# Expert rounds of a fused two-model kernel: even block placement, a last round summed from PSUM, gate rows formed in the convolution stage

## The chip, the cores and the metric

The kernel runs on one core of a Trainium2 chip. The metric is device time in microseconds (us) of the whole program, one launch.

## The reference, cut to what matters

Two transformer-like blocks run one after the other on 256 tokens of width 1024, all in fp32. The second block has two layers. Each layer is a mixer (attention in layer 0, a short convolution in layer 1), and then a mixture of experts with 32 experts in 4 groups, of which each token uses 2. Only the 256 latent tokens are routed here, so each layer has 512 (token, expert) pairs.

```python
x = x + g1 * mixer(modulate(x, ...))
f = modulate(x, norm_ffn_g, sh2, sc2)            # 256 rows of 1024
# _hier_moe: group = argmax(g_prob + b), 2 experts of its 8, weights w
y[token] = sum over its 2 experts e of
           w * ((silu(f @ w_gate[e]) * (f @ w_up[e])) @ w_down[e])
x = x + g2 * y
...
return rmsnorm(x, final_norm_g)                   # after layer 1
```

An expert has three matrices of 2 MB (1024x512, 1024x512, 512x1024), so 6.3 MB an expert and 201 MB a layer. `g1` and `g2` are rows of 1024 gates, the same for all tokens.

## The kernel before, in words

The five engines each have a program of their own, and semaphores tie them together. SyncE (SP) issues the loads of weights, in a fixed order. GpSimd (POOL) issues the gathers and scatters of rows and some small loads. TensorE (PE) multiplies, VectorE (DVE) and ScalarE (ACT) move data from PSUM and do the elementwise work.

**The first block's feed-forward part (`ffn0`)** has 22 steps. In each step TensorE makes an up product (`up`) and the down product of the step before (`down(t - 1)`, which waits for `gated`). VectorE scales, convolves and gates, and then does one `mod_pass`: a pass over a 2 MB chunk of `w_mod`, which POOL loads (`mod_loads`, one chunk ahead of the pass, two buffers).

**Blocks.** Behind the router, the rows of each expert are cut in blocks of 32 slots. Each expert has at least one block. There are 48 blocks (`NB`), three to a round (`WIDE`), so 16 rounds (`ROUNDS`). If the experts need `total` blocks, `48 - total` are free, and expert `e` starts at block

```python
pst[e] = start[e] + ((NB - total) * e >> 5)      # start[e]: blocks of the experts before e
```

which spreads the free blocks by the number of the expert. A free block belongs to the expert before it and holds no rows. `route` computes this on VectorE, in operations of 32 columns that each wait for the one before (L2332 to L2335), from products of TensorE with the counts. A second chain (L2354 to L2358) gives each expert's end on 32 partitions, for the table `tab_i`.

**Rounds (`experts`).** The weights of three experts fit in SBUF (`experts3`, expert `e` in place `e % 3`). SP loads expert by expert in this order: gate matrix of `e`, down matrix of `e - 1`, up matrix of `e`. Each half of a matrix waits (L775) until the last round that uses expert `e - 3` has finished the same half (`quarter_done`). A round multiplies its 96 gathered rows by the gate, up and down matrix of its three blocks, each matrix in four quarters. The first block's weights are read in place, those of the second are copied by VectorE (L2400) and those of the third by ScalarE (L1684). VectorE waits until the matrices of the expert of the third block have landed. Behind the down product VectorE multiplies the 96 rows with the gates `g2` into `ym` (L2408), and POOL scatters them to the DRAM tensor `y_rows` by slot (L2775).

**After the rounds.** SP waits for the last scatter, then fetches `y_rows` into `y01` (`fetch`, L812), and `combine` adds both rows of each token to the residual in 8 operations (L2448, L2449). ScalarE squares each half as it is combined, VectorE sums them (L1962), and the norm goes on. In layer 0 the gate rows of layer 1 are formed at the same place: `row_diags` makes three 128x1024 operands on VectorE (L2213), `row_pair` makes six products on TensorE and six copies on ScalarE (L1656). Then comes the convolution's stage: 8 steps of 24 products on TensorE (L843), and a short chain on VectorE for each.

## Time and profile before

| | |
|---|---|
| Median of 3 runs | 2247.38 us (2246.84 to 2250.01) |
| Profiled execution, its time | 2246.04 us |
| Profiled execution, its span | 2244.2 us |
| TensorE busy | 1929.4 us (86%) |
| VectorE busy | 956.4 us (43%) |
| ScalarE busy | 665.8 us (30%) |
| DMA | 617.69 MB, mean 275 GB/s |
| Rounds of layer 0 | about 1066 to 1554 us |
| Rounds of layer 1 | about 1731 to 2219 us |

The span is the time from the first to the last record of the profiled execution, 1.8 us less than its own time. TensorE's busy time is that of its matmul records, which overlap.

### The profile page before, as it was taken

Reading aid. Unit: us, or ns where it says so; the run is one execution under the profiler, and the core shown is the slowest. Engines: PE = TensorE matmul, PEld = TensorE weight load, DVE = VectorE, ACT = ScalarE, POOL = GpSimd, SP = SyncE. Lnnn points to the kernel's source line nnn. Section 1 sums busy time; section 2 is a strip of 40 time slices with the busy share of each in tenths; the row PEclk is TensorE's granted clock in tenths of the full one; section 3 lists DMA queues with packets and bytes.
Section 4 is the critical chain, followed back from the end, with each engine's and each line's share of the span. In section 5 each row is a group of like instructions: output and inputs, shape, how many; then the busy total and the mean of one; then the engine's idle time right before and its main releaser. Section 6 shows DMA issues by size and latency. Waiting matters only on the chain.

```text
span 2244.2 us, 29502 instructions
## 1 busy us (share of the span) xinstructions
PE 1929.4 (86%) x9453; PEld 1085.2 (48%) x9454; DVE 956.4 (43%) x2077; ACT 665.8 (30%) x1053; POOL 100.0 (4%) x133
## 2 busy tenths in 40 slices
PE   8878999999999999997976887777897967877885
PEld 4534777745577775554432433333764423323332
DVE  2273888312478534444432432334224423323333
ACT  1142000012400002132543543444102534434443
POOL 2000000000000000000000000000000000000000
PEclk9869999999899999998998998999997988888998
DMA  8502898433179543305899999996645999999994
GB/s 282 201 6 99 325 343 312 178 141 143 66 277 358 197 167 132 124 31 207 334 421 383 360 412 407 407 416 260 258 160 221 385 421 379 415 421 389 411 394 166
DMA packets 84611, 617.69 MB, mean 275 GB/s; under 512 B 16289, under 2 KB 16609, under 8 KB 21809
## 3 DMA queue, kind: packets, MB, share of 16 engines
q1 hardware_dynamic: 68912, 544.70, 61.3%
q0 software_dynamic: 14752, 69.77, 8.3%
q10 hardware_dynamic: 864, 2.19, 0.2%
q8 instruction: 44, 0.72, 0.1%
q14 instruction: 39, 0.31, 0.0%
HBM read 621.84 MB, written 19.92 MB: 286 GB/s over the span
## 4 chain that ended last, share of the span: by engine, by line
PE 67%; DMA 19%; DVE 5%; issue 3%; ACT 3%; DVEq 2%; SPq 1%; ACTq 0%; POOLq 0%
PE ps L843 25%; PE ps L1216 15%; PE ps L1053 14%; DMA big<-in_w_up 7%; PE ps L1065 7%; DMA big<-in_w_down 5%; DMA big<-in_w_gate 5%; PE ps L1218 3%; PE ps L857 2%; ACT big L1684 2%; DVEq L2413 1%; DVE hT L2421 1%; PE ps L1245 1%; DMA c_res<-f_rows,big 1%; PE ps L1208 1%
## 5 line engine op out<-in xcount | busy, mean ns | idle before, releaser
L1216 PE MATMUL ps<-big,hT 128*32 128x512 f32 x3072 | 723.5, 627 | 144.0 <-ACT big L1684 140.5
L1218 PE MATMUL ps<-big,hT 128*32 x1536 | 722.3, 627 | 0.0
L1684 ACT COPY big<-big 128x1024 f32 x384 | 395.0, 1046 | 526.2 <-PE ps L1218 267.1
L2400 DVE TENSOR_SCALAR big<-big 128x1024 f32 x384 | 263.0, 696 | 623.0 <-PE ps L1218 375.6
L1216 PEld LDWEIGHTS ps<-big,hT 128*32 128x32 f32 x3072 | 200.5, 114 | 541.3 <-DVE big L2400 276.0
L1053 PE MATMUL ps<-hT,big 128*128 128x256 f32 x1408 | 311.1, 379 | 0.0
L843 PE MATMUL ps<-big,hT 128*128 128x512 f32 (+4 forms) x792 | 299.7, 537 | 4.8 <-DMA big<-in_dense 2.5
L1053 PEld LDWEIGHTS ps<-hT,big 128*128 128x128 f32 x1408 | 266.7, 190 | 49.0 <-issue 14.8
L843 PEld LDWEIGHTS ps<-big,hT 128*128 128x128 f32 x792 | 144.4, 195 | 149.3 <-issue 139.7
L843 PE MATMUL ps<-big 64*30 64x256 f32 (+14 forms) x704 | 161.4, 512 | 30.7 <-DVE big L2350 8.3
L1218 PEld LDWEIGHTS ps<-big,hT 128*32 128x32 f32 x1536 | 164.8, 114 | 6.1 <-issue 0.9
L1065 PE MATMUL ps<-big 128*128 128x512 f32 x352 | 159.2, 595 | 0.4 <-DVE big L2163 0.4
L2173 DVE SCALAR_TENSOR_TENSOR big<-big,s_ccol 128x512 f32<-128x512 f32 x196 | 147.4, 752 | 7.0
L1648 ACT ACTIVATE big<-big 128x256 f32<-128x256 f32 x44 | 18.3, 417 | 363.8 <-DVE big L2155 363.8
L843 PEld LDWEIGHTS ps<-big 64*128 64x128 f32 (+8 forms) x704 | 81.7, 196 | 90.3 <-issue 63.1
L843 PE MATMUL ps<-hT,big 128*128 128x256 f32 (+1 forms) x480 | 112.8, 398 | 1.9 <-ACT hT L1897 1.9
L843 PEld LDWEIGHTS ps<-hT,big 128*128 128x128 f32 x480 | 92.4, 193 | 22.7 <-issue 10.7
L1065 PEld LDWEIGHTS ps<-big 128*128 128x128 f32 x352 | 66.1, 190 | 72.9 <-issue 69.0
L2137 DVE TENSOR_TENSOR big<-ps,big 128x512 f32<-128x512 f32 x44 | 30.4, 690 | 119.5 <-PE ps L1053 117.5
L1245 PE MATMUL ps<-c_ident,hT 96*128 96x96 f32 x128 | 29.5, 318 | 50.4 <-DVE hT L2421 50.4
L857 PE MATMUL ps<-c_ident,big 128*128 128x128 f32 (+4 forms) x349 | 57.4, 301 | 17.6 <-DVE big L2085 10.9
L2764 POOL DMA_INDIRECT c_res<-f_rows,big x32 | 32.5, 1014 | 715.4 <-PE ps L1208 486.7
(333 smaller groups left out, 1176.2 us busy)
## 6 DMA issues: line engine op xcount, KB each, us to landing
big<-in_w_down SPq DMA_DIRECT2D x128, 1024.0 KB
big<-in_w_gate SPq DMA_DIRECT2D x128, 1024.0 KB, 12.1
big<-in_w_up SPq DMA_DIRECT2D x128, 1024.0 KB, 12.9
big<-in_dense SPq DMA_DIRECT2D x52, 1536.0 KB, 8.3
big<-in_dense POOLq DMA_DIRECT2D x28, 2048.0 KB, 9.9
big<-in_dense SPq DMA_DIRECT2D x21, 2048.0 KB, 8.3
big<-in_dense SPq DMA_DIRECT2D x5, 1024.0 KB, 7.5
big<-y_rows SPq DMA_DIRECT2D x4, 1024.0 KB, 6.2
```

Source lines behind the costliest of these rows:

```text
L843: ins = nc.tensor.matmul(out, lhsT, rhs, start=start, stop=stop)
L857: ins = nc.tensor.transpose(out, rows, const["ident"][0:k, 0:k])
L1053: ins = nc.tensor.matmul(ps[:, t % 2, f * S:(f + 1) * S], w[:, k, f * P:(f + 1) * P], hT[:, k, S:2 * S], start=k == 0, stop=k == KT - 1)
L1065: ins = nc.tensor.matmul(ps[:, 4 + 2 * c + h, :], gT[:, t % 2, c * P:(c + 1) * P], w[:, h * BW:(h + 1) * BW], start=t == 0, stop=t == FT - 1)
L1216: nc.tensor.matmul(ps[g * SLOTS:(g + 1) * SLOTS, bank, :], xT[:, k, g * SLOTS:(g + 1) * SLOTS], side[:, g - 1, quarter % 2, at:at + BW], s ...
L1218: return nc.tensor.matmul(ps[0:SLOTS, bank, :], xT[:, k, 0:SLOTS], experts3[:, bass.ds(here, 1), kind * CH + row:kind * CH + row + BW] .re ...
L1245: ins = nc.tensor.transpose(ps[:, 4 + 3 * h, k * ROWS:(k + 1) * ROWS], rows, const["ident"][0:ROWS, 0:ROWS])
L1684: nc.scalar.copy(side[:, 1, quarter % 2, :], experts3[:, bass.ds(there, 1), lo:lo + QW] .rearrange("p a n -> p (a n)")).then_inc(s["side2_ ...
L2137: tt(U[:, par, :, 2:S + 2], ps[:, par, :].rearrange("p (a b) -> p a b", a=2), token_scale, mult)\
L2173: ins = stt(acc, mod_w[j % 2][:, k, :], ccols[:, k, col:col + 1], acc, mult, add)
L2400: ts(side[:, 0, quarter % 2, :], experts3[:, bass.ds(there, 1), lo:lo + QW].rearrange("p a n -> p (a n)"), 1.0, None, mult).then_inc(s["si ...
L2764: nc.gpsimd.indirect_dma_start(out=xe, out_offset=None, in_=f_rows[:, :], in_offset=bass.IndirectOffsetOnAxis(ap=token_i[:, b:b + 1], axis=0),
```

## The change

The diff has four parts.

1. **Even placement.** Expert `e` starts at block `start[e] + min(lead[e], NB - total)`, where `lead[e]` is the largest `3 * e' // 2 - start[e']` over `e' <= e`. So an expert isn't placed ahead of one and a half blocks per expert as long as free blocks are left. The running maximum takes five shifted `max` operations; the second chain becomes one `tensor_tensor_reduce`, and three small products of TensorE go.
2. **Rows of the last round.** 15 rounds are scattered. Their rows are fetched during the last round (the fetch waits for the scatter of round 14 and for the last round's first matrix) and added to the residual. The last round's rows are then written to `ym` in two halves, multiplied by a one-hot matrix `hot` (four products), and added from PSUM. Since some rows of `y_rows` are no longer written, there is one tensor per layer, and both are filled with zeros in `ffn0`: eight writes of 512 KB by POOL, which waits for them before it goes on to `mod_loads`.
3. **Gate rows** of layer 1 are formed in steps 0 to 2 of the convolution's stage, whose products now use 6 PSUM banks; `row_diags` comes after the scaling of the stage's input.
4. The loads of `conv_in` stand behind the fetch in SP's order and so can be issued during the last round too. `final_g` is loaded after the last round's second matrix.

```diff
-    r[:, 1] = e
-    r[:, 2] = (np.arange(P) + 1)[:, None]
+    r[:, 1] = WIDE * e // 2
+    r[np.arange(E - 1), 2, e[1:]] = 1.0
+    r[E - 1, 2, E - 1] = 2 * NB
...
@@ fetch (SP)
-                after(sp, "moe" + tag)
+                sp.wait_ge(m["y_stored"].sem, m["y_stored"].end)
+                sp.wait_ge(m["quarter_done"].sem, m["quarter_done"].at(12 * (ROUNDS - 1) + 4))
...
@@ route (PE)
-                mm(ps[0:E, 4, 0:1], rt[0:E, 0, :], nbT[0:E, 0:1], True, False)
-                mm(ps[0:E, 4, 0:1], const["ident"][0:E, 0:E], nbT[0:E, 0:1], False, True)
-                mm(ps[0:E, 4, 1:2], const["ones"][0:E, 0:E], nbT[0:E, 0:1], True, True, s["route_pe"].sem)
...
@@ experts (PE), after the last turn
+                pe.wait_ge(m["hot_ready"].sem, m["hot_ready"].end)
+                for c in range(T):
+                    for h in range(2):
+                        if c == 0:
+                            pe.wait_ge(m["last_ready"].sem, m["last_ready"].at(h + 1))
+                        mm(ps[:, 2 * c + h, :], hot[0:ROWS, c, :], ym[0:ROWS, h * BW:(h + 1) * BW], True, True,
+                           m["last_spread"].sem)
...
@@ between the expert stage and normX2 (PE), and in conv
-            for j in range(3):
-                row_pair("g1_1", j, 2 * j)
-            after(pe, "g1_1")
...
+                if t < 3:
+                    if t:
+                        g = st["g1_1"]["gate_copied"]
+                        pe.wait_ge(g.sem, g.at(2 * t))
+                    row_pair("g1_1", t, CONV_BANKS)
...
@@ ffn (DVE), ffn0 alone
+                if name == "ffn0":
+                    nc.vector.memset(zeros, 0.0).then_inc(st["zero"]["zeros_ready"].sem, 1)
...
@@ route (DVE)
-                L(ts(rest[:, 0:E], ps[:, 3, E:2 * E], -1.0, float(NB), mult, add))
-                L(tt(pad_i[:, 0:E], rest[:, 0:E], rt[:, 1, :], mult))
-                L(ts(pad_i[:, 0:E], pad_i[:, 0:E], E.bit_length() - 1, None, ALU.logical_shift_right))
-                L(tt(pst, ps[:, 3, 0:E], pad_i[:, 0:E], add))
+                first = SHIFTS[-1]
+                ts(rest, ps[:, 3, E:E + 1], -1.0, float(NB), mult, add)
+                L(tt(lead[:, 0, first:], rt[:, 1, :], ps[:, 3, 0:E], sub))
+                for i, n in enumerate(SHIFTS):
+                    old, new = lead[:, i % 2, :], lead[:, 1 - i % 2, :]
+                    L(tt(new[:, first:], old[:, first:], old[:, first - n:first - n + E], ALU.max))
+                L(stt(pst, lead[:, len(SHIFTS) % 2, first:], rest, ps[:, 3, 0:E], ALU.min, add))
...
@@ experts (DVE), after the last turn; combine() goes
-                rows_out(ROUNDS - 1)
+                link(v, nc.vector.tensor_copy(last_token, token_i[:, ROUNDS - 1:ROUNDS]))
                 for c in range(T):
+                    ins = ts(hot[0:ROWS, c, :], const["iota"][0:ROWS, :], float(c * P), last_token[0:ROWS, :], add, ALU.is_equal)
+                ins.then_inc(m["hot_ready"].sem, 1)
+                if layer == 0:
+                    mod_gains(1, 0)
+                for out, c, h in parts:
+                    if h == 0:
+                        v.wait_ge(m[f"y_fetched_{c}"].sem, m[f"y_fetched_{c}"].end)
+                    link(v, tt(out, out, y01[:, c, 0, h * BW:(h + 1) * BW], add))
+                    link(v, tt(out, out, y01[:, c, 1, h * BW:(h + 1) * BW], add))
+                v.wait_ge(done.sem, done.end)
+                v.wait_ge(s["y_stored"].sem, s["y_stored"].end)
+                for h in range(2):
+                    cols = slice(h * BW, (h + 1) * BW)
+                    tt(ym[0:ROWS, cols], ps[0:ROWS, 5 + h, :], gb2[0:ROWS, 0, cols], mult).then_inc(m["last_ready"].sem, 1)
+                for i, (out, c, h) in enumerate(parts):
+                    v.wait_ge(m["last_spread"].sem, m["last_spread"].at(i + 1))
+                    tt(out, out, ps[:, 2 * c + h, :], add).then_inc(m["combined"].sem, 1)
...
@@ POOL
+            s = st["zero"]
+            pool.wait_ge(s["zeros_ready"].sem, s["zeros_ready"].end)
+            for l in range(DEPTH):
+                for q in range(4):
+                    pool.dma_start(y_rows[l][q * P:(q + 1) * P, :], zeros).then_inc(s["rows_zeroed"].sem, 16)
+            pool.wait_ge(s["rows_zeroed"].sem, s["rows_zeroed"].end)
             mod_loads(0, "normF0")
```

## Rows read from the trace of the kernel before

**Rows 1.** Stretches of layer 0's rounds: length, busy by engine, TensorE clock, DMA share, GB/s

```profile
1190.00:1224.00 34.00, 27.24 (x165) 11.40 (x162) 10.87 (x17) 13.61 (x15) 2.01 (x2) 0.87 0.92 359
...
1276.00:1289.00 13.00, 11.51 (x84) 5.42 (x78) 5.96 (x8) 7.73 (x8) 1.01 (x1) 1.00 0.60 202
1289.00:1397.00 108.00, 84.45 (x526) 37.30 (x525) 35.60 (x55) 45.46 (x51) 7.06 (x7) 0.91 1.01 415
...
1538.00:1554.00 16.00, 14.76 (x100) 7.39 (x94) 5.44 (x9) 7.25 (x8) 0.00 (x0) 1.00 0.10 41
```

**Rows 2.** The same view, rounds of layer 1

```profile
1856.00:1889.00 33.00, 26.81 (x161) 10.91 (x158) 10.10 (x16) 13.62 (x15) 2.00 (x2) 0.87 0.91 347
...
2031.00:2062.00 31.00, 25.44 (x162) 10.82 (x159) 10.63 (x17) 13.67 (x16) 1.06 (x2) 0.93 0.95 366
...
2200.00:2219.00 19.00, 17.75 (x125) 8.95 (x118) 7.52 (x12) 9.93 (x10) 0.00 (x0) 1.00 0.07 29
```

**Rows 3.** Order of time, SP's loads of expert weights around 1282 us

```profile
1282.81 3.75 SPq L767 DMA_DIRECT2D big<-in_w_gate  x2
```

**Rows 4.** Order of time, VectorE, L2408 (start, duration): ends of rounds

```profile
1254.43 1.22 DVE L2408 TENSOR_TENSOR c_res<-ps,hT 96x1024 f32<-96x1024 f32 x1
...
1279.07 1.21 DVE L2408 TENSOR_TENSOR c_res<-ps,hT 96x1024 f32<-96x1024 f32 x1
...
2171.68 1.21 DVE L2408 TENSOR_TENSOR c_res<-ps,hT 96x1024 f32<-96x1024 f32 x1
...
2196.51 1.21 DVE L2408 TENSOR_TENSOR c_res<-ps,hT 96x1024 f32<-96x1024 f32 x1
...
2219.53 1.22 DVE L2408 TENSOR_TENSOR c_res<-ps,hT 96x1024 f32<-96x1024 f32 x1 [2.63 <-PE ps L1218]
```

**Rows 5.** Order of time, layer 0, from the last round to the norm

```profile
1550.82 0.69 DVE L2400 TENSOR_SCALAR big<-big 128x1024 f32 x1 [1.02 <-PE ps L1218]
...
1554.14 1.22 DVE L2408 TENSOR_TENSOR c_res<-ps,hT 96x1024 f32<-96x1024 f32 x1 [2.63 <-PE ps L1218]
...
1564.20 0.69 DVE L2448 TENSOR_TENSOR x_res<-x_res,big 128x512 f32<-128x512 f32 x1 [0.83 <-DMA big<-y_rows]
...
1572.73 0.16 DVE L1962 TENSOR_TENSOR sums<-ssq_x 128x2 f32<-128x2 f32 x1 [2.49 <-ACT big L1565]
```

**Rows 6.** Order of time, layer 1, the same sum

```profile
2237.12 0.16 DVE L1962 TENSOR_TENSOR sums<-ssq_x 128x2 f32<-128x2 f32 x1 [0.79 <-ACT big L1565]
```

**Rows 7.** By stretch, as rows 1: after the rounds of layer 0

```profile
1554.00:1560.00 6.00, 0.11 (x1) 0.00 (x0) 1.79 (x3) 0.00 (x0) 1.10 (x2) 0.79 0.03 10
...
1562.00:1564.00 2.00, 2.00 (x4) 0.96 (x3) 1.34 (x3) 0.59 (x1) 0.09 (x1) 0.50 1.01 410
```

**Rows 8.** Groups of TensorE instructions, 1577 to 1665 us (convolution)

```profile
L843 PE MATMUL ps<-hT,big 128*128 128x256 f32 x384 | 84.9, 385 | 1.9 <-ACT hT L1897 1.9
```

**Rows 9.** Order of time, route, layer 0

```profile
1049.33 0.19 DVE L2335 TENSOR_TENSOR big<-ps,big 128x32 f32<-128x32 f32 x1
1049.55 0.22 DVE L2337 SCALAR_TENSOR_TENSOR big<-big,ps 128x64 f32<-128x64 f32 x1
```

**Rows 10.** Order of time, ffn0, VectorE: mod pass 1, gate of step 2

```profile
240.34 0.48 DVE L2171 TENSOR_SCALAR big<-big,s_ccol 128x512 f32<-128x512 f32 x1
...
249.38 0.43 DVE L2163 TENSOR_TENSOR big<-big 128x256 f32<-128x256 f32 x1
```

**Rows 11.** Chain that ended last, in order of time: ffn0 (start, duration)

```profile
254.54 3.43 PE ps L1065 x8
```

**Rows 12.** The page, DMA issues: count, KB each, median us to landing

```profile
big<-in_dense POOLq DMA_DIRECT2D x28, 2048.0 KB, 9.9
...
f_rows<-big ACTq DMA_DIRECT2D x4, 512.0 KB, 8.3
...
out_x<-x_res SPq DMA_DIRECT2D x2, 512.0 KB, 2.7
```

**Rows 13.** Order of time, ffn0, POOL: load of mod chunk 2

```profile
237.23 0.54 POOL L2786 DMA_DIRECT2D big<-in_dense  x1 [16.70 <-DVE big L2173]
```

More of the change, by code:

```diff
@@ L209, in two_blocks @@
         f_rows = nc.dram_tensor("f_rows", [S, D], fp32, kind="Internal").ap()
-        y_rows = nc.dram_tensor("y_rows", [2 * S, D], fp32, kind="Internal").ap()
+        y_rows = [nc.dram_tensor(f"y_rows{l}", [2 * S, D], fp32, kind="Internal").ap() for l in range(DEPTH)]
         def area(lo, *shape, parts=P):
@@ L387, in two_blocks @@
         side = area(3 * CH, 2, 2, QW)
-        y01 = area(2048, TC, 2, D)
+        y01 = area(0, TC, 2, D)
+        hot = hflat[:, 3584:3584 + TC * P].rearrange("p (c n) -> p c n", c=TC)
+        last_token = hflat[:, 3584 + TC * P:3584 + TC * P + 1]
+        zeros = area(6144, D)
         gb2 = hflat[:, 2560:2560 + D].rearrange("p (a d) -> p a d", a=1)
@@ L422, in two_blocks @@
         nbT = area(RB + 1768, P)
-        rest = area(RB + 1896, E + 1)
-        pad_i = area(RB + 1929, E + 1).bitcast(i32)
+        SHIFTS = tuple(1 << i for i in range(E.bit_length() - 1))
+        lead = area(RB + 2680, 2, SHIFTS[-1] + E)
+        rest = area(RB + 2776, 1)
+        next_at = area(RB + 1896, E)
         pst = area(RB + 1962, E)
@@ L1164, in route @@
                 e = st["ent" + name[-1]]
-                pe.wait_ge(g2["diag_done"].sem, g2["diag_done"].end)
+                pe.wait_ge(g2["gate_diags"].sem, g2["gate_diags"].end)
                 pe.wait_ge(e["turned_a"].sem, e["turned_a"].end)
                 for h in range(2):
-                    mm(ps[:, 7 - h, :], const["ones"][:], diag2[:, 4 * h:4 * h + 4, :], True, True, g2["banks_ready"].sem)
+                    mm(ps[:, 7 - h, :], const["ones"][:], diag2[:, 4 * h:4 * h + 4, :], True, True, g2["gate_ready"].sem)
                 pe.wait_ge(s["route_dve"].sem, s["route_dve"].at(4))
@@ L1791, in _ @@
             ffn("ffn0")
+            after(act, "zero")
             s = st["normA1"]
@@ L1887, in _ @@
             after(act, "moe0")
-            for j in range(3):
-                row_pair("g1_1", j, 2 * j)
-            after(act, "g1_1")
             combined_squares("comb0", "normX2")
             root("normX2", rstd_x)
-            token_scales("normX2", 6)
+            token_scales("normX2", 2)
             s = st["normX2"]
@@ L2219, in entry @@
                 g1, g2 = st["g1_" + tag], st["g2_" + tag]
-                v.wait_ge(g1["act_evac"].sem, g1["act_evac"].end)
+                v.wait_ge(g1["gate_copied"].sem, g1["gate_copied"].end)
                 tt(diag2, const["ident"][:].unsqueeze(1).broadcast_to([P, KT, P]),
-                   mod[:, layer, 5 * KT:6 * KT, 0].unsqueeze(2).broadcast_to([P, KT, P]), mult).then_inc(g2["diag_done"].sem, 1)
+                   mod[:, layer, 5 * KT:6 * KT, 0].unsqueeze(2).broadcast_to([P, KT, P]), mult).then_inc(g2["gate_diags"].sem, 1)
                 v.wait_ge(r["aux_loaded"].sem, r["aux_loaded"].end)
@@ L2226, in entry @@
                 nc.vector.tensor_reduce(swS, swK.rearrange("p k n -> p n k"), AX.X, add).then_inc(r["route_dve"].sem, 1)
+                nc.vector.memset(lead[:, :, 0:SHIFTS[-1]], 0.0)
                 nc.vector.tensor_copy(vals[:, :, 1], const["tokid"][:])
@@ L2351, in route @@
                 ins.then_inc(step, 1)
+                L(nc.vector.tensor_tensor_reduce(out=next_at[0:E, :], in0=pst[0:E, :], in1=rt[0:E, 2, :], scale=1.0,
+                                                 scalar=0.0, op0=mult, op1=add, accum_out=pend[0:E, :]))
+                ts(past[0:E, :], const["iota"][0:E, 0:NB], pend[0:E, :], None, ALU.is_ge).then_inc(step, 1)
                 v.wait_ge(s["route_pe"].sem, s["route_pe"].at(7))
[L2354 to L2359 removed]
                 nc.vector.tensor_copy(slot_w, ps[:, 6, 2 * ROUNDS:3 * ROUNDS])
@@ L2437, in experts @@
                     turn(b)
-                rows_out(ROUNDS - 1)
-            def combine(name, T, x):
-                s = st[name]
+                m = st["comb" + name[-1]]
+                parts = [(lat(c)[:, h * BW:(h + 1) * BW], c, h) for c in range(T) for h in range(2)]
+                link(v, nc.vector.tensor_copy(last_token, token_i[:, ROUNDS - 1:ROUNDS]))
                 for c in range(T):
-                    v.wait_ge(s[f"y_fetched_{c}"].sem, s[f"y_fetched_{c}"].end)
-                    for h in range(2):
-                        cols = slice(h * BW, (h + 1) * BW)
-                        out = x(c)[:, cols]
-                        link(v, tt(out, out, y01[:, c, 0, cols], add))
-                        tt(out, out, y01[:, c, 1, cols], add).then_inc(s["combined"].sem, 1)
+                    ins = ts(hot[0:ROWS, c, :], const["iota"][0:ROWS, :], float(c * P), last_token[0:ROWS, :], add, ALU.is_equal)
[15 more added lines that the diff above has]
+                    tt(out, out, ps[:, 2 * c + h, :], add).then_inc(m["combined"].sem, 1)
             gains = small["gcols"][:].rearrange("p (i k) -> p i k", k=KT)
@@ L2552, in _ @@
             ffn("ffn0", "normF0")
+            after(v, "zero")
             for h in range(2):
@@ L2818, in _ @@
             moe("moe0", "1", 1)
-            after(pool, "moe1")
+            d = st["moe1"]["quarter_done"]
+            pool.wait_ge(d.sem, d.at(12 * (ROUNDS - 1) + 8))
             aux("final", [(fg_row, dram["final_g"])])
```

76 lines of the change are left out of this document (39 added, 37 removed).

## The prediction

> **What bounds the kernel now.** I read the busy times by stretch first. In the rounds of both layers DMA is the bound: between 1289 and 1397 us its share is 1.01 and it moves 415 GB/s, while TensorE's records cover 84 of 108 us [rows 1]. A round needs two new experts on average (32 experts, 16 rounds), 12.6 MB of weights and 0.8 MB of rows. At 415 GB/s that is 32 us. A round whose weights are there takes 24.6 us: from 1254.43 to 1279.07 [rows 4]. So the end of a layer is the time at which DMA is through, plus a tail, and something inside the rounds is worth time only where it fills a hole of DMA or shortens the tail.
>
> The same view shows the holes. In layer 0 the share is 0.92 for 34 us and 0.60 for 13 us, which against 1.01 is 34 x 0.09 = 3.1 and 13 x 0.41 = 5.3, together 8.4 us [rows 1]. In layer 1 it is 0.91 for 33 us and 0.95 for 31 us, 3.3 + 1.9 = 5.2 us [rows 2]. The order of SP's loads tells what a hole is: the gate matrix issued at 1282.81 [rows 3] comes at the second quarter of the round that began at 1279 [rows 4], when the queue had run dry. All three places for experts were taken, and none was free before that round.
>
> The tails: DMA is through at about 1539.5 in layer 0 (share 0.10 from 1538 to 1554) [rows 1], and the last product ends at 1554.1 [rows 5], so 14.6 us. In layer 1 it is through at about 2200 (0.07) [rows 2], and the last product ends at 2219.5 [rows 4], so 19.5 us.
>
> Last I read the chain and the order of time around the places that change: from the last round to the norm [rows 5, 6], the convolution [rows 8], and `ffn0` [rows 10, 11].
>
> **Even placement.** The routing isn't in the trace, so I ran the reference's router on its inputs: 36 blocks are needed in either layer, 12 are free; layer 0 has one expert of three blocks and two of two, layer 1 has four of two. By the old rule 3 rounds of layer 0 and 10 of layer 1 reach beyond expert 2r + 1 in round r (one of layer 1 by two experts), so three new or nearly new experts meet in one round, and another round needs only one. By the new rule no round of either layer does. While a round uses three experts all places are taken and SP can only follow TensorE by the quarter; with two, the third place takes loads a round ahead (five matrices, 25 us of DMA at 415 GB/s, can be queued behind a gate matrix). I take the holes as filled by four fifths: of 8.4 + 5.2 = 13.6, 11 us. The bound below is nothing: another hole can open, for instance where layer 0 now has the rounds (12, 12, 12) and (13, 14, 15). Above it is all 13.6 and some 3 us of smaller holes.
>
> The tail of layer 1 is a second gain. Its last two rounds ran at the pace of the engines, 24.8 and 23.0 us [rows 4], behind a round that had to wait for expert 28's down matrix (26, 27, 28). It becomes (26, 27, 27), and the last round can start when expert 31's gate matrix lands, as in layer 0. I take layer 0's tail, 14.6 for 19.5: 5 us, between 0 and 5. Together **-16** (0 to -22).
>
> **Route.** On VectorE four linked operations of 32 columns become an unlinked one and seven linked ones. From 1049.33 to 1049.55 is one link, 0.22 us [rows 9]. So 7 x 0.22 + 0.1 - 4 x 0.22 = 0.76 us a layer, in front of the first gather, which the first round waits for. The second chain and the three products lay beside TensorE's 128-column products and are worth nothing; put ahead of the wait, the reduce stays in the same cover. **+1.5** for both layers (0 if the gather's wait behind expert 2's weights hides it, 2 at most).
>
> **Rows of the last round.** Before, in layer 0: last product 1554.1, scatter, fetch, first add at 1564.20, sum of squares at 1572.73 [rows 5]. Now VectorE's queue counts. Its last copy of weights ends at 1551.5 [rows 5]; then come the token copy and two one-hot rows (0.7), the gains (0.4) and eight adds of 0.72 (5.8), to 1558.4. These lie partly behind the last product, so the multiplication with the gates starts 4.3 us later than it did: what was hidden behind a fetch is late next. It takes two halves of 0.65 (half of L2408's 1.21 [rows 4]), and the first product starts at 1559.2. A product of 256 columns is two instructions of 0.22 us (84.9 / 384) [rows 8]; one of 512 columns costs twice that, 0.88 us, at full clock. But TensorE has been idle since 1554. Before, with the same idle stretch, the granted clock was 0.79 over 1554 to 1560 and 0.50, 1.2 GHz, when it worked again [rows 7]; at that level a product costs 1.76. I take two at either level, 5.3 us, to 1564.5, then the last add (0.7) and the squares (0.8): sum at 1566.0 instead of 1572.73, **-6.7**. In layer 1 the last copy ends 2.6 us ahead of 2219.5, at 2216.9, and there are no gains to form: 2216.9 + 0.7 + 5.8 + 0.7 + 5.3 + 0.7 + 0.8 = 2230.9, rounded up to 2231.1 for the waits, instead of 2237.12 [rows 6], **-6.0**. All at full clock each would gain 1.8 more, all at half 1.8 less. The fetch has the time: round 14's rows are stored some 10 us into the last round, and 2 MB at 415 GB/s are 5 us.
>
> The Trainium skill ("TensorE: Matmul & The Clock Gate", part 1) states that an idle array falls to 1.2 GHz and comes back to 2.4 GHz after it has been kept busy. By that rule four short products behind an idle stretch may all run at 1.2 GHz, and the two sums would be -4.9 and -4.2; by the full level they would be -8.5 and -7.8. The trace agrees with the fall: 0.50 [rows 7].
>
> **Gate rows.** Before, their six products lay beside the fetch. Now they stand in the stream of TensorE in the convolution, which waited 1.9 us in all in 384 instructions and 84.9 us [rows 8]: it is the bound there. 6 x 0.88 = **+5.3** (7 if a pair waits for its copies). VectorE's three operations and ScalarE's six copies lie in gaps, since each has one short chain per step of 10.6 us (84.9 / 8). `conv_in`'s earlier loads are worth nothing, as no product waited for one.
>
> **Zeros in `ffn0`.** The 128x1024 memset is hidden: VectorE waits there for ScalarE. Eight writes of 512 KB, 4.2 MB, stand on POOL's queue ahead of mod chunk 1, whose pass started at 240.34 [rows 10]. They start at about 224.5, behind `convw` (which lands sooner without the chunk beside it). At 415 GB/s they take 10 us, and with 2 us of latency are there at 236.5. Then chunk 1 (2 MB) shares the engines with a 1.5 MB chunk of SP, 9.9 us to landing as the median of its kind [rows 12], at about 246.5 to 248. So pass 1 and all VectorE has queued behind it come 6 to 8 us late. The cover is TensorE's own lag: gate 2 is done at 249.8 [rows 10], and `down(2)` starts at 254.54 [rows 11], so 4.7 us are free, and the rest is paid, 1.3 to 3.3; VectorE then catches up again. I take **+3** (0 to 8). Chunk 2 was issued at 237.23 [rows 13] and now comes right behind chunk 1, no later than its pass needs it.
>
> The writes' rate is the unknown. The nearest rows: `out_x`, 512 KB in 2.7 us on a quiet queue, and `f_rows`, 512 KB in 8.3 us beside expert 2's weights [rows 12]. I stay with the first, because DMA is nearly idle here. The Trainium skill ("DMA: Bandwidth & Descriptors", "Issuing engines are not separate DMA queues") states that transfers of all issuing engines interleave on the same 16 DMA engines. It speaks against a free fill: zeros also push back SP's chunks. With only `out_x`'s rate the sum is +3; with a full SP queue in their way it would be nearer +5.
>
> **The sum.** -16 + 1.5 - 6.7 - 6.0 + 5.3 + 3 = -18.9 us, against the profiled execution's own 2246.04 (span 2244.2 and 1.8 around it): 2227.1. The median shown is 1.3 above that execution: 2247.4 - 18.9 = 2228.5.
>
> **Rivals.**
> - *The holes only move.* A DMA queue of three places may be dry as often by the new rule, because a place is freed a round later for every second expert. For it: the first rounds, the same by both rules, have holes too. Against: the large holes lie where the old rule is uneven. Then -16 becomes 0 to -4, say -2: 2242.5. Chance 0.17.
> - *The zeros are the bound* (the slower side). One mechanism: POOL waits for all eight writes, and `f_rows`' rate, 8 x 8.3 = 66 us in series, holds chunk 1 until 224.5 + 66 + 9.9 = 300, 60 us late; less 4.7 of cover is 55 paid, 52 more than assumed: 2280. It decides from where the fill takes 19 us more than I say, some 31 us, where 18.9 are used up. Against: nothing else is in flight. Chance 0.07.
> - *A better case*: all holes, clock at full in the products, zeros covered. -22 + 1 - 8.5 - 7.8 + 5.3 + 0 = -32: 2215. Chance 0.11.
> - The forecast has 0.65. Its own range is 2219 to 2237.
>
> A measurement of this kernel can tell about 0.2%, 4.5 us, from no change. The first rival straddles that bound: half of it counts as same. Faster is 0.65 + 0.11 + 0.08 = 0.84, less 0.02 for a small miss of several terms: 0.82; same 0.10; slower 0.08. The range for 8 in 10, from the better case to the first rival: 2215 to 2243.
>
> **What would show it.** Two windows over the rounds of either layer should have a DMA share of 1.0 without a stretch under 0.9, and the ends of rounds should come 31 to 32 us apart in the middle. Layer 1's last round should end 15 us behind the last weights. From the last product to the first norm's sum 11 to 12 us instead of 18.6. The convolution's TensorE time should be 90 us. In `ffn0`, the second pass should start near 247, with one wait of TensorE of 1 to 4 us for `gated`, and none after it. The prediction is wrong if DMA's holes are as large as before, or if that one wait is over 10 us.

## The result, and the profile after

The changed kernel took 2254.26 us (median of 9 runs, 2245.79 to 2259.35) and the kernel before 2246.84 (9 runs on the same chip, 2240.77 to 2250.01): ratio 1.0033, 95% interval 1.0017 to 1.0048. It is slower by 0.33%, 7.4 us, where 2228.5 was forecast. The profiled execution has a span of 2252.4 us, 8.2 more than before.

I compared the two traces place by place. The first is the order of time of the changed kernel in `ffn0`, for the chain that ended last:

```profile
224.12 2.98 POOL y_rows L2836 x6
...
227.84 9.04 DMA y_rows<-big
236.88 0.28 issue
237.16 9.82 DMA big<-in_dense
246.98 0.02 issue
247.01 0.50 DVE big L2193
```

The fill lands at 236.88, 0.4 us from where it was forecast. But mod chunk 1 is issued only then and lands 9.82 later, so VectorE begins pass 1 at 247.01. Here are the same wait on VectorE, and the loads on POOL's queue:

```profile
247.01 0.49 DVE L2193 TENSOR_SCALAR big<-big,s_ccol 128x512 f32<-128x512 f32 x1 [9.33 <-DMA big<-in_dense]
```

```profile
224.12 4.25 POOL L2836 DMA_DIRECT2D y_rows<-big  x8 [6.87 <-DVE big L2149]
237.16 1.06 POOL L2819 DMA_DIRECT2D big<-in_dense  x2 [8.79 <-DMA y_rows<-big]
```

`ffn0` ends at 463.05 instead of 457.78, although it began 2.75 us earlier (in stages that the change doesn't touch): it is 8.0 us longer, for a forecast of 3. The `down(2)` that waited shows a second price: it took 6.7 us instead of 3.43 [rows 11]. TensorE's granted clock was 0.53 meanwhile, after the wait of 4.74 us, where it was 1.00 from 254.5 to 258 in the kernel before.

```profile
256.53 6.71 PE L1076 MATMUL ps<-big 128*128 128x512 f32 x8 [4.74 <-DVE big L2185]
```

```profile
256.50:263.00 6.50, 6.47 (x8) 2.71 (x9) 6.24 (x9) 0.00 (x0) 0.32 (x1) 0.53 0.69 258
```

Then the rounds, as stretches (busy by engine, TensorE clock, DMA share, GB/s), changed kernel:

```profile
1184.00:1216.00 32.00, 25.02 (x156) 11.38 (x156) 10.36 (x17) 13.51 (x16) 2.01 (x2) 0.95 1.01 420
1276.00:1289.00 13.00, 7.92 (x38) 3.24 (x41) 3.81 (x5) 4.09 (x4) 1.00 (x1) 0.59 0.36 134
...
1279.00:1286.00 7.00, 4.92 (x18) 1.96 (x21) 3.12 (x4) 3.00 (x3) 1.00 (x1) 0.50 0.29 121
...
1290.00:1398.00 108.00, 84.37 (x527) 36.89 (x521) 34.26 (x52) 45.39 (x50) 6.03 (x6) 0.94 1.01 413
1541.00:1543.00 2.00, 2.00 (x18) 1.08 (x15) 1.05 (x2) 1.39 (x2) 0.65 (x1) 1.00 0.56 221
1543.00:1545.00 2.00, 2.00 (x18) 0.89 (x12) 0.03 (x1) 0.36 (x1) 0.00 (x0) 1.00 0.20 84
1545.00:1548.00 3.00, 0.62 (x6) 0.00 (x0) 0.00 (x0) 0.06 (x1) 0.00 (x0) 1.00 0.19 79
```

Against [rows 1], the early hole of layer 0 is gone (1.01 where it was 0.92), and the one around 1280 is larger (0.36 for 0.60), in the rounds (12, 12, 12) and (13, 14, 15). For 7 us of it the share is 0.29, between four and five of 16 engines. The new thing is the end. The share doesn't fall to nothing: it is 0.20 and 0.19 for five microseconds, three of 16 engines. And VectorE waits for what they bring:

```profile
1548.10 1.30 DVE L2423 TENSOR_SCALAR big<-big 128x1024 f32 x2 [5.06 <-DMA big<-in_w_up]
```

The same is seen in layer 1, with two engines. A stretch of the changed kernel, and VectorE's groups from the first to the last end of a round in layer 0:

```profile
2214.00:2216.00 2.00, 2.00 (x15) 0.78 (x11) 0.00 (x0) 0.00 (x0) 0.00 (x0) 1.00 0.12 51
```

```profile
L2423 DVE TENSOR_SCALAR big<-big 128x1024 f32 x168 | 114.9, 697 | 279.4 <-PE ps L1226 153.0 <-DMA big<-in_w_up 52.7 <-DMA big<-in_w_gate 44.3
```

The page, DMA issues: the median from issue to landing of a weight half has doubled. First the changed kernel, then the kernel before (whose page has no figure for the down matrix):

```profile
big<-in_w_down SPq DMA_DIRECT2D x128, 1024.0 KB, 24.8
big<-in_w_gate SPq DMA_DIRECT2D x128, 1024.0 KB, 25.7
big<-in_w_up SPq DMA_DIRECT2D x128, 1024.0 KB, 25.1
```

```profile
big<-in_w_gate SPq DMA_DIRECT2D x128, 1024.0 KB, 12.1
big<-in_w_up SPq DMA_DIRECT2D x128, 1024.0 KB, 12.9
```

Read together: the queue is deep and most engines are full, as forecast. But a load has landed when the last of its 16 engines is through, and two or three engines lag. (The doubled median isn't itself a sign of the lag. It goes with the even placement: 11.9 us for the gate matrices in `e2_old_place` below, but 22.7 in `e4_quiet`, which has almost no row transfers.) The rounds did not get shorter. VectorE's `rows_out` marks their ends:

```profile
1101.50 1.22 DVE L2431 TENSOR_TENSOR c_res<-ps,hT 96x1024 f32<-96x1024 f32 x1
...
1538.65 1.21 DVE L2431 TENSOR_TENSOR c_res<-ps,hT 96x1024 f32<-96x1024 f32 x1
...
1770.61 1.21 DVE L2431 TENSOR_TENSOR c_res<-ps,hT 96x1024 f32<-96x1024 f32 x1
...
2209.07 1.21 DVE L2431 TENSOR_TENSOR c_res<-ps,hT 96x1024 f32<-96x1024 f32 x1
```

From the first such end to the 15th it is 437.2 us in layer 0 and 438.5 in layer 1; before it was 435.1 and 438.4. I call the sum of the two the *rounds' time* below: 875.7, before 873.5.

Last, the two ends of layers, order of time, changed kernel. Layer 0 in the first fence, layer 1 in the second:

```profile
1563.85 0.69 DVE L2423 TENSOR_SCALAR big<-big 128x1024 f32 x1 [1.02 <-PE ps L1226]
...
1571.24 1.28 DVE L2479 TENSOR_TENSOR c_res<-ps,hT 96x512 f32<-96x512 f32 x2
...
1572.08 6.00 PE L854 MATMUL ps<-c_res,hT 96*128 96x512 f32 x8 [4.94 <-DVE c_res L2479]
...
1579.69 0.16 DVE L1982 TENSOR_TENSOR sums<-ssq_x 128x2 f32<-128x2 f32 x1 [0.89 <-ACT big L1585]
```

```profile
2237.56 1.28 DVE L2479 TENSOR_TENSOR c_res<-ps,hT 96x512 f32<-96x512 f32 x2
...
2238.39 5.37 PE L854 MATMUL ps<-c_res,hT 96*128 96x512 f32 x8 [4.54 <-DVE c_res L2479]
...
2245.37 0.16 DVE L1982 TENSOR_TENSOR sums<-ssq_x 128x2 f32<-128x2 f32 x1 [0.89 <-ACT big L1585]
```

From the last copy's end (1564.54) to the sum of squares it is 15.15 us, before 21.2 [rows 5]. This part works as forecast. And the convolution, TensorE's groups from 1584 to 1679 us:

```profile
L854 PE MATMUL ps<-hT,big 128*128 128x256 f32 x384 | 86.6, 389 | 1.9 <-ACT hT L1915 1.9
L854 PE MATMUL ps<-big,c_ones 128*128 128x512 f32 x12 | 5.6, 592 | 0.0
```

### The profile page after: what moved, and what is told of

Read it like the earlier page. It is cut to its first block, busy times and chain, and to the rows that moved or that the text cites. A ratio compares the mean times of both kernels' runs of the same rounds, so it can differ in the third digit from the quotient of the medians.

```text
span 2252.4 us, 29544 instructions
## 1 busy us (share of the span) xinstructions
PE 1953.4 (87%) x9457; PEld 1097.9 (49%) x9458; DVE 963.4 (43%) x2100; ACT 664.7 (30%) x1053; POOL 101.6 (5%) x139
## 4 chain that ended last, share of the span: by engine, by line
PE 59%; DMA 30%; DVE 5%; issue 3%; ACT 3%; DVEq 1%; SPq 0%; POOL 0%; ACTq 0%; POOLq 0%
PE ps L854 26%; DMA big<-in_w_up 25%; PE ps L1064 12%; PE ps L1224 9%; PE ps L1076 6%; PE ps L1226 2%; PE ps L868 2%; ACT big L1704 2%; DMA big<-in_w_down 2%; DMA big<-in_w_gate 1%; DMA big<-in_dense 1%; DMA c_res<-f_rows,big 1%; DMA y_rows<-big 0%; DVE big L2086 0%; DVEq L2436 0%
## 5 line engine op out<-in xcount | busy, mean ns | idle before, releaser
L1224 PE MATMUL ps<-big,hT 128*32 128x512 f32 x3072 | 738.0, 636 | 145.8 <-ACT big L1704 144.0
L1226 PE MATMUL ps<-big,hT 128*32 x1536 | 736.7, 636 | 0.0
L1224 PEld LDWEIGHTS ps<-big,hT 128*32 128x32 f32 x3072 | 204.6, 116 | 547.0 <-DVE big L2423 275.1
L854 PE MATMUL ps<-big 64*30 64x256 f32 (+14 forms) x700 | 155.7, 501 | 34.8 <-issue 17.7
L1226 PEld LDWEIGHTS ps<-big,hT 128*32 128x32 f32 x1536 | 167.2, 116 | 8.1
L854 PEld LDWEIGHTS ps<-big 128*128 128x128 f32 (+8 forms) x700 | 79.3, 191 | 91.7 <-issue 71.8
L854 PEld LDWEIGHTS ps<-hT,big 128*128 128x128 f32 x480 | 93.3, 195 | 24.1 <-issue 11.9
```

What stands on the lines that cost most here:

```text
L854: ins = nc.tensor.matmul(out, lhsT, rhs, start=start, stop=stop)
L1224: nc.tensor.matmul(ps[g * SLOTS:(g + 1) * SLOTS, bank, :], xT[:, k, g * SLOTS:(g + 1) * SLOTS], side[:, g - 1, quarter % 2, at:at + BW], s ...
L1226: return nc.tensor.matmul(ps[0:SLOTS, bank, :], xT[:, k, 0:SLOTS], experts3[:, bass.ds(here, 1), kind * CH + row:kind * CH + row + BW] .re ...
```

## The experiments

Each kernel was measured beside the kernel before on the same chip, and ratios are to that. Differences to "changed" are to its median above, 2254.3 us; beside all of these kernels, the one before took 2246.1 to 2247.7 us.

**Parts of the change**

`e1_zeros_spread`:

```diff
-for l in range(DEPTH): for q in range(4): pool.dma_start(y_rows[l][...], zeros)
-pool.wait_ge(s["rows_zeroed"].sem, s["rows_zeroed"].end)
-mod_loads(0, "normF0")
+# in mod_loads, after mod_load(layer, j), j = 2 to 9: one of the eight writes
+pool.wait_ge(s["rows_zeroed"].sem, s["rows_zeroed"].end)      # behind the last load
```

> The changed kernel with each of the eight writes of zeros issued after one of the modulation chunks 2 to 9 instead of all ahead of chunk 1, and with no wait for their landing there. Theory A (the fill holds up modulation chunk 1, issued at 237.16 in the changed kernel behind the wait for the zeros, and the first feed-forward stage with it): the stage gives back what it lost, 8 us, so 2246 us, 0.4% faster than the changed kernel; pass 1 of the modulation starts within 1 us of where it did in the kernel before, counted from the stage's start. Rival B (it is the traffic of the zeros, 4.2 MB, that costs the time, wherever it stands): no change, 2254 us.

2247.07 us, ratio 1.0003 (0.9992 to 1.0015): 7.2 us less than the changed kernel. VectorE's queue in this kernel shows pass 1 with no wait, on time:

```profile
237.34 0.48 DVE L2193 TENSOR_SCALAR big<-big,s_ccol 128x512 f32<-128x512 f32 x1
246.89 0.49 DVE L2193 TENSOR_SCALAR big<-big,s_ccol 128x512 f32<-128x512 f32 x1
```

`ffn0` takes 238.2 us in this trace, as in the kernel before. So the fill costs by its place in front of chunk 1, and its traffic shows no cost here.

`e2_old_place` and `e3_even_alone`:

```diff
-    r[:, 1] = WIDE * e // 2          # e2: in the changed kernel, back to
+    r[:, 1] = e                      # (rest * e) >> 5 spare blocks ahead of e
# e3: in the kernel before, the other way round, with the new chain of maxima
```

> The changed kernel with the old placement rule (a share of the spare blocks ahead of each expert) and all else as changed. Theory A (a weight half has landed only when the last of the 16 DMA engines is through, two or three of them are slower than the others, and these are busy all through the rounds with either rule except for 3 us of layer 0; so the placement moves nothing): 2251 us, between 2246 and 2255. Rival B (the mean share of the DMA engines paces the rounds, as forecast, and something else in the change ate the gain): the 16 us come back as a loss, 2270 us. Rival C (the even rule itself slows the rounds by the 4.6 and 1.8 us that they got longer): 2248 us.

> The kernel before with the even placement and its route arithmetic alone; rows, sums and gate rows as before. Theory A (slow DMA engines pace the rounds): within 4 us of the kernel before, 2243 to 2251 us, and the median landing of the weight halves doubles from 12 to about 25 us as in the changed kernel. Rival B (mean share paces): 2231 us. Rival C (the even rule slows the rounds by itself): 2253 us.

e2: 2245.55 us, 0.9994 (0.9983 to 1.0006). e3: 2253.97 us, 1.0033 (1.0022 to 1.0043). The even rule costs 8.7 us in the changed kernel and 7.9 in the kernel before: rival C, whose 2248 and 2253 us are the nearest forecasts. My theory that the placement moves nothing fell, and with it the idea that some engines are slow whatever is done. The rule makes them slow.

**The row transfers**

`e4_quiet` and `e15_no_scatter`:

```diff
 gather(0); gather(1)
-for b in range(ROUNDS): gather(b + 2); ...; scatter(b)
+scatter(0)                                      # e4: no other row transfers
+for b in range(ROUNDS): gather(b + 2)           # e15: all gathers, scatter(0)
```

> The changed kernel without the row transfers of the rounds beyond the first: rounds 2 to 15 use the rows gathered for round 1, and the rows of rounds 1 to 14 are not scattered (that part of the computation is left out). Theory A (two or three DMA engines are slower because they also serve the row transfers of the software queue): with these gone the slow engines catch up, the pitch of the rounds falls from 32.2 towards the 30.7 us that the mean share gives, up to 1.5 us times 15 rounds times two layers, 45 us, so 2210 us. Rival B (these engines are slower by themselves): the pitch stays at 32 us and the time within 5 us of 2254.

> The changed kernel without the scatters of rounds 1 to 14 (their rows are left out of the sum), all gathers kept. The quiet kernel, without gathers and scatters from round 2 on, was 64.6 us faster. If each transfer of a row costs its slow engine the same, whichever way it goes: half of that, 2222 us (2217 to 2227). If only the writes to memory are dear: 2195 us. If only the gathers are: 2250 us.

e4: 2189.64 us, 0.9741 (0.9723 to 0.9758), 64.6 us less than changed, where theory A had 45 at most. e15: 2219.62 us, 0.9884 (0.9870 to 0.9899), 34.6 less, as forecast for an equal price either way. So it is the row transfers, read and write alike, although they move only 4 KB a valid row, 4 MB a layer, 2% of the weights.

**Which slots the rows lie in**

```diff
 # slot n of a block of 32 holds row ...            (changed: row n)
+n -> 16 * (n % 2) + n // 2                          # e5: every second slot
+n -> 4 * (n // 8) + n % 4 + 16 * (n % 8 // 4)       # e12: fours
+n -> 4 * (n % 8) + n // 8                           # e13: eight slots apart
-out=xe ... in_=ym                                   # e6: transfers of 96 rows
+out=xe[0:ROWS, :] ... in_=ym[0:ROWS, :]
```

> The changed kernel with the rows of each block of 32 dealt to every second slot (the first 16 go to slots 0, 2, ..., 30), so that a block's valid rows, some 16 of 32, no longer lie side by side. Theory A (the row transfers are dealt to the DMA engines by stretches of neighbouring rows, so the first rows of each block always fall to the same few engines; these are the slow ones, and the even rule, which puts a dummy block third in nearly every round, loads them most): the slow engines carry half of that, and the rounds get shorter by 8 to 15 us in each layer, 2225 to 2238 us. Rival B (rows are dealt to the engines in turn, row by row): every second slot then concentrates them on half of the engines, and the time is 2265 to 2290 us. Rival C (the slow engines are slow by themselves, or by the count of descriptors): 2254 us.

> The changed kernel with the first 16 rows of a block dealt to slots 0 to 3, 8 to 11, 16 to 19 and 24 to 27. Twelve more small comparisons a layer cost 2 us in both. Theory A with stretches of eight rows to an engine (128 rows, 16 engines): each stretch has four valid rows, as with every second slot, 2231 us. Rival D (rows dealt to the engines in another way, in turn over 16 or in stretches of four or fewer, where every second slot helped by its step of two): little or nothing gained, 2245 us or more.

> The changed kernel with consecutive rows of a block dealt to slots eight apart (row r of a block to slot 8 x (r mod 4) + r div 4). Model 1 (an engine serves a stretch of eight slots): four engines share the rows of each block evenly however few they are, the most loaded one falls from 160 row transfers a layer (every second slot) to about 110, and the time is at or below that of every second slot, 2215 to 2229 us. Model 2 (pairs of neighbouring slots go to one engine, in turn over 16; fits the fours, which gained nothing): the rows pile up on few engines, slower than the changed kernel, over 2262 us. Model 3 (stretches of four in turn over 16, fits them as well): counts as in the changed kernel, 2254 us.

> The changed kernel with gathers and scatters of 96 rows, those in use, instead of 128 with 32 that are never valid. Theory A: 6 rows instead of 8 fall to an engine, so the slowest carries at most three quarters of what it did and all 16 take part; shorter by 4 to 8 us in each layer, 2238 to 2246 us. Rival B (dealt in turn): a slow engine had 8 rows of which the valid ones are spread evenly already; within 3 us of 2254. Rival C (it is the count of descriptors): a quarter fewer of them, 2 to 4 us in each layer, 2247 to 2250 us.

e5: 2228.93 us, 0.9924 (0.9902 to 0.9946), 25.3 less than changed, as theory A has it. e12: 2254.82, 1.0039 (1.0025 to 1.0054), nothing gained, though by stretches of eight slots each engine would have what it has in e5. e13: 2232.71, 0.9947 (0.9934 to 0.9960), by none of the three models. e6: 2258.04, 1.0044 (1.0027 to 1.0061), 3.8 above the changed kernel's median, with intervals that overlap, and outside all three forecasts. So it matters where the rows lie, but not as in my model.

The combinations and the kernel before with every second slot:

> The changed kernel (even placement) with the zeros spread over the modulation chunks, every second slot, and 96 rows a transfer. Theory A: 7 us from the zeros and 12 to 18 us in each layer, 2211 to 2223 us. Rival B: over 2255 us. Rival C: 2240 to 2247 us.

> As e7_even_both, but with the old placement. Theory A: with the row transfers spread over the engines by the slots the old rule has no advantage left, and its holes (13.6 us of them in the kernel before) come out: 8 to 16 us slower than e7_even_both. Rival B and C (the advantage of the old rule, 8 us, has nothing to do with which engine serves which row): 8 us faster than e7_even_both.

> The changed kernel with every second slot and the zeros spread over the modulation chunks, 128 rows a transfer. If the two add up (25 us for the slots, 7 us for the zeros): 2222 us, between 2218 and 2226. If the longer packets with 96-row transfers, 409 to 411 GB/s in place of 417 to 421 at the same share, are noise: as with them, 2225 us.

> The same with the old placement. Theory A (the old rule's advantage was only that its dummy blocks change place and so move the row transfers to other engines): the even rule is now ahead, by 3 to 8 us, 2225 to 2230 us. Rival C (the even rule slows the rounds by itself): the old rule stays 8 us ahead, 2214 us.

> The kernel before with every second slot alone. Theory A: with the old placement the slow engines carry less of the row transfers than with the even one, so the gain is about half of the 25 us: 8 to 15 us, 2232 to 2239 us. Rival (the gain of the slots belongs to something of the changed kernel): 2247 us.

> As e13_eights with the zeros spread over the modulation chunks: 7 us less than it, whatever that is; by model 1, 2208 to 2222 us, at or below e9_even_slots (2223.3).

e7: 2225.19 us, 0.9902 (0.9877 to 0.9927). e8: 2230.19, 0.9922 (0.9905 to 0.9938). e9: 2223.29, 0.9886 (0.9869 to 0.9904). e10: 2228.88, 0.9916 (0.9898 to 0.9935). e11: 2231.44, 0.9921 (0.9904 to 0.9938). e14: 2227.82, 0.9922 (0.9907 to 0.9937), 4.5 above e9 and so outside what model 1 gave. With the slots spread, the even rule is ahead of the old one (by 5.6 us in e9 against e10, intervals overlapping), where it was 8 behind. e9 and e10 lie in their ranges. e7 and e11 lie just outside theirs (2.2 above and 0.6 below), and e8 is 5.0 slower than e7, where 8 to 16 was given.

**The dealing, read packet by packet.** The trace's DMA records have a start, a length and a size for each packet. A weight packet (8 KB) takes 0.31 us and a row (4 KB) 0.16; a skipped row leaves 4 bytes. A round of layer 0 has four valid rows in its first block, five in its second and none in the third. These are the starts of its nine row packets in the gather, in us from the start of each stretch:

```
changed  (from 1267.7): 0.83 1.29 1.76 1.85 2.23 2.69 3.15 3.62 3.78
fours    (from 1264.8): 0.83 1.30 1.74 1.78 2.24 2.71 3.17 3.34 3.80
eights   (from 1260.0): 0.60 0.64 0.65 0.81 1.93 2.03 2.07 2.07 2.54
```

In the first two lines eight rows come 0.47 us apart or closer, a weight packet and a row in turn (0.31 + 0.16), so on one engine, and one comes beside them. That engine has the four rows of the first block *and* four of the second. The ninth is the second block's fifth row. In the third line, where consecutive rows are eight slots apart, four rows start side by side, then four more, then the ninth. The records don't name their engines, but the three lines and the times of the kernels below fit one dealing (the scatter of this round shows the same pattern, 0.46 us apart, with one of its nine records missing): engine k (0 to 7) serves slots 4k to 4k + 3 of the first and of the second block, and engine 8 + k those of the third (and of the 32 slots that are never used). The Trainium skill ("DMA: Bandwidth & Descriptors", "The descriptor swizzle") states this dealing, for a transfer to 128 partitions; the trace agrees.

With the router's counts of rows per block this gives each engine's row transfers in a layer (per round `min(v1, 4) + min(v2, 4)` for engine 0 and rows packed; two for each row, gather and scatter, one in the last round). For the most loaded engine, and the rounds' time of the profiled execution:

```
kernel                 transfers L0 + L1    rounds' time   812.4 + 0.1281 x transfers
e4  quiet                     0                812.4           (anchor)
e15 no scatters             124 + 123          843.1           844.1
e5  every second slot       164 + 174          855.9           855.7
e13 eights                  188 + 186          857.3           860.3
e12 fours                   248 + 246          874.0           875.7
changed                     248 + 246          875.7           (anchor)
e3  even rule alone         248 + 246          874.3           875.7
before                      192 + 192          873.5           861.6
e2  old rule, changed       192 + 192          874.1           861.6
e11 before, second slots    124 + 132          857.0           845.2
```

The line goes through the quiet and the changed kernel (63.3 us / 494). All with the even rule lie within 3 us of it. Those with the old rule lie 12 us above. I read that as their holes; no run shows the holes apart. I predicted three more kernels from such a line, with layer 0's slope (437.2 - 405.1 = 32.1 us for 248 transfers, 0.129 each):

```diff
+n -> 8 * (n % 4) + n // 4               # e16, e18: consecutive rows four slots apart
-    r[:, 1] = WIDE * e // 2             # e16, e17: dummy block second, not third
+    r[:, 1] = (WIDE * e + 1) // 2
```

> The changed kernel with the zeros spread, consecutive rows dealt to slots four apart (row r of a block to slot 4 x (r mod 8) + r div 8), and the even rule shifted so that the dummy block is the second of a round and not the third. Theory E (engine k of 0 to 7 serves slots 4k to 4k+3 of the first and of the second block, engine 8+k those of the third, as the transfer of nine rows shows where eight follow one another on one engine; first to last y rows take 405 us + 0.129 us for each row transfer of the most loaded engine): the most loaded engine has 84 and 81 row transfers in the two layers instead of 248 and 246, so 0.129 x 329 = 42 us less than with the zeros spread alone (2247.1): 2205 us, between 2200 and 2212. Rival F (something else than the most loaded engine sets the pace, and every second slot, 2223 us with the zeros spread, is the floor): 2219 to 2227 us.

> The changed kernel with the dummy block second instead of third in each round, and nothing else (one constant: target 3e/2 rounded up instead of down). Theory E: the two blocks with rows are now served by different engines, 156 and 150 transfers on the most loaded one instead of 248 and 246, 24 us less: 2230 us, between 2225 and 2236. Rival F: the placement's holes and ends are the same, so 2254 us.

> The changed kernel with the zeros spread and rows four slots apart, dummy block third as in the change. Theory E: 135 and 136 transfers on the most loaded engine, 0.129 x 223 = 29 us less than the zeros spread alone: 2218 us, between 2214 and 2223. Rival F: as with every second slot, 2223 us or more.

e17: 2229.08 us, 0.9924 (0.9904 to 0.9943), for 2230 forecast. Nothing but one constant differs from the changed kernel, and by the experts per round it is the worse placement: two rounds of each layer now have three different experts, where one of layer 0 had. e18: 2217.84, 0.9880 (0.9864 to 0.9896), for 2218. e16: 2210.05, 0.9839 (0.9822 to 0.9857), for 2205. Their rounds' times are 853.2, 847.4 and 839.6; the line gives 851.6, 847.1 and 833.5. These are the marks of e16 in layer 1, 415.1 us apart (438.5 in the changed kernel), and a stretch of that layer:

```profile
1744.03 1.21 DVE L2434 TENSOR_TENSOR c_res<-ps,hT 96x1024 f32<-96x1024 f32 x1
...
2159.14 1.21 DVE L2434 TENSOR_TENSOR c_res<-ps,hT 96x1024 f32<-96x1024 f32 x1
```

```profile
1790.00:2150.00 360.00, 287.65 (x1835) 126.38 (x1830) 124.21 (x189) 161.01 (x177) 23.04 (x23) 0.95 1.01 420
```

The same stretch of the changed kernel has the same share at a lower rate. So little of all this does the mean show:

```profile
1790.00:2150.00 360.00, 289.48 (x1779) 128.00 (x1774) 120.79 (x182) 155.10 (x170) 23.06 (x23) 0.91 1.01 412
```

e16 is the fastest kernel of the study: 36.6 us below the kernel before.

## Why the prediction was wrong

**The step that failed is "Even placement", -16.** It measured +7.9 (e3). What failed is the premise of its first part, that the end of a layer is the time at which DMA's *mean* is through. With the rows of a round in the first two blocks, engines 0 to 7 serve nearly all of them, and the most loaded one has 248 + 246 transfers instead of 192 + 192. By the line the 110 more cost 0.128 x 110 = 14.1 us, and they eat what the even rule gives back. That is about 12 us, the distance of the old rule's rounds from the line, near the 11 that I took for the holes. (Without the line: e11, old rule, 256 transfers, is 9.6 us longer than e18, even rule, 271.) The old rule had moved its dummy blocks about, and so, without being meant to, the rows between the two groups of engines.

**In the changed kernel the holes were not filled.** These are the rounds of layers 0 and 1, first of the kernel before, then of the changed one:

```profile
1093.00:1528.00 435.00, 345.07 (x2186) 152.48 (x2188) 148.34 (x225) 191.64 (x211) 27.73 (x27) 0.93 0.99 403
1758.00:2196.00 438.00, 345.99 (x2184) 152.00 (x2184) 148.05 (x225) 191.31 (x210) 27.13 (x27) 0.91 1.00 405
```

```profile
1102.00:1539.00 437.00, 348.03 (x2189) 155.10 (x2186) 147.65 (x225) 191.18 (x211) 27.31 (x27) 0.93 0.99 407
1771.00:2209.00 438.00, 355.24 (x2187) 157.60 (x2183) 147.63 (x224) 190.65 (x211) 27.08 (x27) 0.91 1.00 406
```

The share is 0.99 and 1.00 in both, and "holes as large as before" was the sign of being wrong that the prediction gave. The hole around 1280 is, by the rows, in large part the lag: most engines stand still while four or five work. At the same place e18, with the same placement and the rows spread, has this:

```profile
1267.00:1273.00 6.00, 6.00 (x39) 2.48 (x36) 1.39 (x2) 2.10 (x2) 1.01 (x1) 0.86 0.72 274
```

**The tail of layer 1** was to gain 5. The last round (15th to 16th end, e3 against before) took 28.7 us instead of 23.0 in layer 1 and 28.0 instead of 26.0 in layer 0. These 7.7 us are nearly all of the loss in e3's trace; the rounds up to the 15th are 0.8 longer (874.3 for 873.5). The most loaded engine comes in last, and the last round waits for it, as the 5.06 us at 1548.10 show. The gain was also read too large: layer 0's tail was counted from 1539.5, behind what DMA still moved after 1538, layer 1's from 2200 itself. Read alike (0.07 of 19 us), layer 1's is 18.2, and 3.6 us were there to gain, not 5.

**Row traffic** was counted by bytes, 0.8 MB a round for the sum over 16 engines. By bytes it is even less, since only valid rows move. Its price goes by the one engine that has most of them; leaving nearly all of it out gave 64.6 us (e4).

**Zeros, +3**: the mechanism was right (chunk 1 behind the fill, pass 1 at 247 as forecast), only the size was off: 7.2 us (e1), 8.0 in the trace. Pass 1 came 9.4 us late against the stage's start (247.01 + 2.75 - 240.34), where I had said 6 to 8, the cover was 4.7, and the product behind the wait ran 3.3 us longer, at the granted clock of 0.53, which I had left out. TensorE's wait for `gated` was 4.74 us, where I had given 1 to 4. The range that I gave, 0 to 8, held it. The rival of the slow fill is out: the fill took 12.8 us (224.12 to 236.88), not 31.

**Last round's rows, -6.7 and -6.0**: by the trace -6.6 (from the last copy of weights to the convolution) and -6.1 (in layer 1, from that copy, 2231.26 instead of 2216.89, to the sum of squares). The products took 6.00 and 5.37 us, where I had two of four at half clock and 5.3. The granted clock over these stretches of the changed kernel was 0.60 and 0.66:

```profile
1572.00:1578.00 6.00, 5.92 (x9) 2.60 (x10) 2.59 (x4) 1.47 (x5) 0.00 (x0) 0.60 1.01 415
2238.00:2243.00 5.00, 4.61 (x7) 2.01 (x8) 2.28 (x5) 1.37 (x4) 0.00 (x0) 0.66 0.00 0
```

**Gate rows, +5.3**: +6.4 in the trace (from the convolution's first product to that of the next stage, 93.9 us for 87.5). The twelve instructions cover 5.6 us; the 384 others took 86.6 instead of 84.9, which I can't assign, so TensorE's products took 92.2 us for a forecast of 90. **Route, +1.5**: 0.8 us in layer 0, as forecast.

With what was measured the sum is 7.9 (route included) - 6.6 - 6.1 + 6.4 + 7.2 = +8.8, for a measured 7.4 with an interval of 3.8 to 10.8.

**The rivals.** "The holes only move" was nearest in its number, and holes did move. But its reason, a queue that runs dry because a place is freed a round later, isn't what the runs show: with the same placement and the rows spread (e18) the share over the rounds is 1.01 in both layers. None of my rivals asked whether all 16 engines have the same to do, though the kernel before already shows a share of 0.17 behind the last full stretch, which is not quite three engines:

```profile
1541.00:1543.00 2.00, 2.00 (x17) 1.13 (x17) 0.69 (x1) 1.05 (x1) 0.00 (x0) 1.00 0.17 66
```

**What stays open.** The slope, 0.13 us a transfer, is below the 0.16 us of a row packet. Part of it is the count: the quiet kernel still has the transfers of rounds 0 and 1 (24 a layer on that engine, mostly ahead of the first mark), and e15 has 136 + 135 with the scatter of round 0 and the gather of the last round; with these the slope is 0.142. The rest may be slack in the loads that are ahead, which no run shows. In e16 and e17 layer 0 took 424.5 and 430.1 us, 9 and 5 above what their transfers give by layer 0's own two anchors (405.1 + 0.129 a transfer), and layer 1 took 415.1 and 423.1, 3 less than by its own (407.4 + 0.126 a transfer). The round (3, 4, 5) that the shifted rule makes in layer 0 can be a part: in e16 it is 2.8 us longer than in e18. With every second slot, the rounds' times of transfers of 96 rows are longer than of 128 (860.1 in e7 for 853.9 in e9, 867.0 in e8 for 857.5 in e10), which the count of transfers doesn't explain and the medians hardly show (+1.9 and +1.3). Whether the rounds (12, 12, 12) and (13, 14, 15) can be avoided was not tried.

## What to carry to other kernels

A DMA share of 1.0 is a mean over 16 engines, and a load lands with the slowest. When a stage is bound by DMA, count for each engine what it has, row by row, before filling holes of the mean. The sign here was a share that stood at 2/16 or 3/16 for some microseconds at the end of a stage. Rows of an indirect transfer should lie so that the valid ones are spread over the engines: one change of an index constant was worth 25 us here (e17), more than the 18.9 us that the whole change was to bring. And a fill that is cheap in bandwidth is dear in front of a load that somebody waits for.

## What was unexpected in the hardware

- Gathers and scatters of the rounds cost up to 65 us of 2254 (e4) for 2% of the bytes. 37 of them came back when the same rows were spread over the engines (2210.05 in e16 for 2247.07 in e1).
- Transfers of 96 rows instead of 128 made nothing faster (e6 +3.8 us; e7 against e9 +1.9; both within the intervals). The mean share is as full, at a slightly lower rate: these are stretches of e6 and of the changed kernel, layer 0.

```profile
1110.00:1530.00 420.00, 329.36 (x2080) 144.35 (x2074) 139.75 (x213) 181.78 (x200) 25.82 (x26) 0.93 1.00 405
```

```profile
1110.00:1530.00 420.00, 332.28 (x2084) 148.46 (x2082) 140.68 (x214) 182.48 (x203) 26.17 (x26) 0.93 0.99 409
```

- At a share of 0.19 and 0.20, three engines' worth, DMA moved 79 and 84 GB/s, 26 for each busy engine, no more than its part of the full rate (420 / 16 = 26): here an engine that lagged didn't catch up when the others were done.
